# Softmax attention on one core: two heads' logits issued together on 64 array rows each, two masked blocks merged, one output bank

## The reference, cut to what matters

```python
for each head h, for q in blocks of 64 tokens:
    s_s = q[h] @ k_sel.T * scale + bias[h];   o_s = masked_softmax(s_s) @ v_sel
    s_w = q[h] @ k_win.T * scale + bias[h];   o_w = masked_softmax(s_w) @ v_win
    y[h] = gate0 * o_c + gate1 * o_s + gate2 * o_w
# second block, 8 heads
    y2[h] = masked_softmax(q2[h] @ k2[h].T * scale) @ v2[h]
```

## Time and profile before

| | |
|---|---|
| median of 3 runs | 2138.66 us (2137.55 to 2139.3) |
| time of the profiled execution | 2139.25 us |
| its span, first to last instruction | 2137.4 us |
| PE busy in the span | 1762.5 us (82%) |
| DVE, ACT, POOL busy | 757.8, 482.0, 224.2 us |
| mean granted TensorE clock | 0.909 of full speed |
| selected block, from POOL's first copy to DVE's last addition | 309.7 to 365.3 us |
| window block, likewise | 365.7 to 423.2 us |
| moba block | 1401.0 to 1455.0 us |

### The profile page before, as it was taken

One profiled execution on the slowest core, in us unless ns is written; L12 is line 12 of the kernel. 1 busy time (PEld: TensorE's weight loads), 2 busy tenths in 40 slices (PEclk: granted clock), 3 DMA queues, 4 the chain that ended last, 5 costly groups with the idle time before them and its releaser, 6 DMA issues. The chain is left out here.

```text
span 2137.4 us, 21540 instructions
## 1 busy us (share of the span) xinstructions
PE 1762.5 (82%) x8022; PEld 1175.6 (55%) x8023; DVE 757.8 (35%) x1353; ACT 482.0 (23%) x804; POOL 224.2 (10%) x280
## 2 busy tenths in 40 slices
PE   4979998897778799979978996577539999998873
PEld 2768876755333677868866885356433333333331
DVE  6335225522453677323342122753241111111113
ACT  3212334433000322222222223342101011100001
POOL 4010001000102122200030000010201111110011
PEclk9999999989989899989999995788859999999996
DMA  9312210001560577222221320001909998799994
GB/s 285 111 59 79 87 52 1 1 0 52 204 231 22 207 250 254 80 79 98 98 79 59 99 79 1 1 0 59 361 16 392 425 425 333 315 425 427 426 424 171
DMA packets 99669, 361.52 MB, mean 169 GB/s; under 512 B 21239, under 2 KB 23459, under 8 KB 87275
## 3 DMA queue, kind: packets, MB, share of 16 engines
q1 hardware_dynamic: 90791, 344.48, 42.5%
q0 software_dynamic: 5760, 9.02, 1.2%
q10 hardware_dynamic: 3012, 6.59, 0.8%
HBM read 357.28 MB, written 14.75 MB: 174 GB/s over the span
## 5 line engine op out<-in xcount | busy, mean ns | idle before, releaser
L2299 PE MATMUL x_gpa<-x_ring,x_Ta 128*64 128x512 f32 x608 | 145.9, 636 | 17.6 <-DMA x_ring<-in_w_expert_gate_dram 16.0
L2299 PE MATMUL x_upa<-x_ring,x_Ta 128*64 128x512 f32 x608 | 139.0, 611 | 15.7 <-DMA x_ring<-in_w_expert_up_dram 15.7
L2299 PEld LDWEIGHTS x_gpa<-x_ring,x_Ta 128*64 128x64 f32 x608 | 49.1, 146 | 111.9 <-issue 111.8
L2299 PEld LDWEIGHTS x_upa<-x_ring,x_Ta 128*64 128x64 f32 x608 | 47.5, 141 | 105.2 <-issue 105.2
L317 DVE TENSOR_TENSOR p_lo<-p_raw,p_hi 128x2048 fp32r<-128x2048 f32 x18 | 41.3, 2292 | 145.3 <-ACT p_hi L670 145.3
L324 PE MATMUL fr_p<-p_hi,u_high 128*128 128x512 f32 x224 | 89.1, 398 | 0.0
L325 PE MATMUL fr_p<-p_lo,u_high 128*128 128x512 f32 x224 | 88.0, 393 | 0.0
L326 PE MATMUL fr_p<-p_hi,u_low 128*128 128x512 f32 x224 | 88.0, 393 | 0.0
L2320 PE MATMUL x_y0a<-x_ring,x_aTa 128*64 128x512 f32 x304 | 69.4, 598 | 6.2 <-ACT x_aTa L2360 3.6
L2355 ACT ACTIVATE x_siga<-x_gpa 128x512 f32<-128x512 f32 x19 | 11.3, 597 | 265.5 <-PE x_gpa L2299 265.5
L2320 PE MATMUL x_y1a<-x_ring,x_aTa 128*64 128x512 f32 x304 | 68.6, 592 | 0.0
(11 more groups left out here) (1008 smaller groups left out, 3881.4 us busy)
## 6 DMA issues: line engine op xcount, KB each, us to landing
x_ring<-in_w_expert_gate_dram SPq DMA_DIRECT2D x32, 2048.0 KB, 24.6
x_ring<-in_w_expert_up_dram SPq DMA_DIRECT2D x32, 2048.0 KB, 31.4
x_ring<-in_w_expert_down_dram SPq DMA_DIRECT2D x32, 2048.0 KB, 29.9
p_raw<-in_w_in_dram SPq DMA_DIRECT2D x18, 1024.0 KB, 5.1
adaw0m<-in_w_ada_dram SPq DMA_DIRECT2D x6, 2048.0 KB, 10.4
adaw1m<-in_w_ada_dram SPq DMA_DIRECT2D x6, 2048.0 KB, 9.7
fr_ada<-in_ada_w_dram SPq DMA_DIRECT2D x4, 2048.0 KB, 16.8
w_raw0m<-in_mlp_w_dram SPq DMA_DIRECT2D x8, 1024.0 KB
```

Source lines behind the costliest of these rows:

```text
L2299: mm = nc.tensor.matmul(ps[CAP * f:CAP * f + CAP, :], self.xT[:, k, CAP * f:CAP * f + CAP], w[m + f][:, k, :], start=(k == 0), stop=(k == ...
```

## The change

A new class `HeadPairs` takes the place of `Heads` in `softmax_attention` (the mLSTM stage keeps `Heads`).

- **Logits by pairs.** The scores of both heads of a unit are issued in one go, in the order of `PAIR_ORDER`, each over its own 64 rows of queries and keys, so that one head's matmuls use array rows 0 to 63 and the other's 64 to 127. Five banks hold the eight results; two of them share bank 4, and `shared` keeps the second of these behind the first. One semaphore step at the end of the pair says that all logits are there. The scores of pair p+1 are issued behind the first head of pair p and wait until all logits of pair p are read.
- **One block for both masked kinds.** The selected and the window branch are two `Branch` entries of one call: four heads in a unit, with queries and bias staged once for both.
- **One bank for outputs.** The outputs of the two heads lie in halves of one bank `ops`; the first weigh of a head waits until DVE has read the outputs of the head before (`out_read`).
- **Finish.** Reciprocal and gate are issued ahead of the wait for the last weigh.
- PE's program is written out for all units instead of a hardware loop.

```diff
+PAIR_BANK = [lambda h: 2 + h, lambda h: 4, lambda h: 2 + h, lambda h: h]
+PAIR_COL = [lambda h: 384, lambda h: 256 * h, lambda h: 0, lambda h: 0]
+
+PAIR_ORDER = [(0, 1), (1, 3), (0, 3), (1, 2), (0, 2), (1, 0), (1, 1), (0, 0)]
...
+class HeadPairs:
...
+        self.sps = [s.bank(f"sps{j}{tag}") for j in range(5)]
+        self.tps = [s.bank(f"tps{j}{tag}") for j in range(2)]
+        self.ops = s.bank(f"ops{tag}")
...
+        def scores(pair, i, first=False):
+
+            if not first:
+                pe.wait_ge(self.scores_read, 8 * pair)
+            for h, j in PAIR_ORDER:
+                r = slice(64 * h, 64 * h + 64)
+                if (h, j) == (1, 1):
+                    pe.wait_ge(self.shared, pair + 1)
+                mm = nc.tensor.matmul(self.logits_of(h, j), self.qst[r, P * j:P * j + P], self.keys_now(i, h, P * (j + 1))[r, :],
+                                      start=True, stop=True)
+                if (h, j) == (0, 1):
+                    mm.then_inc(self.shared, 1)
+            mm.then_inc(self.scores_ready, 1)
...
+        def weigh(n, h, i, br, j):
+            if j == 0:
+                pe.wait_ge(self.out_read, n + 1)
...
+        def unit(i, last):
+            for k, br in enumerate(self.branches):
+                pair = nb * i + k
+                head(2 * pair, 0, i, br)
+                if k + 1 < nb:
+                    self.keys_now = self.branches[k + 1].keys
+                    scores(pair + 1, i)
+                elif not last:
+                    self.keys_now = self.branches[0].keys
+                    pe.wait_ge(self.q_staged, i + 2)
+                    scores(pair + 1, i + 1)
+                head(2 * pair + 1, 1, i, br)
...
-def softmax_attention(nc, C, tag, qT, keys, values, out, units=4, bias=None, gate=None, add=False):
+def softmax_attention(nc, C, tag, qT, branches, units=4, bias=None):
...
+                def coefs(n, h, i, br):
                     ch = Chain(dve, own, n * links)
+                    dve.wait_ge(H.probs_ready, 4 * n + 4)
+                    dve.wait_ge(H.turned, 4 * n + 12)
+                    ch.link(nc.vector.reciprocal(coef[h][:, :], sums[h][:, :]))
+                    if gate:
+                        ch.link(nc.vector.tensor_tensor(coef[h][:, :], coef[h][:, :], br.gate(h, i), ALU.mult))
+                    return ch
+
+                def finish(n, h, i, br, pair):
+                    ch = coefs(n, h, i, br)
                     dve.wait_ge(H.weighed, 4 * n + 6)
...
+                    o = H.ops[:, 256 * h:256 * h + NT * HD].rearrange("p (t d) -> p t d", d=HD)
+                    to = tmp[:, :, :] if add else br.out(h, i)
+                    nc.vector.tensor_tensor(to, o, bcast(coef[h][:, :], HD), ALU.mult).then_inc(H.out_read, 1)
                     if add:
...
+                        dve.wait_ge(H.out_read, n + 2)
+                        ch.link(nc.vector.tensor_tensor(br.out(h, i), br.out(h, i), tmp[:, :, :], ALU.add))
                     assert ch.n == links
 
                 def rounds(now, nxt):
                     for j in range(NT):
                         if nxt:
-                            logits(nxt[0], nxt[1], j)
+                            if j == 0 and nxt[1] == 0:
+                                dve.wait_ge(H.scores_ready, nxt[4] + 1)
+                            logits(nxt[0], nxt[1], nxt[2], j)
...
-                        for tag, kz, branch in (("sl", B.ksz, 1), ("wn", B.kwz, 2)):
...
+                        softmax_attention(nc, C, "sw", lambda i: B.qT[:, bass.ds(i, 1), :].rearrange("p a n -> p (a n)"),
+                                          [branch(B.ksz, 1), branch(B.kwz, 2)],
+                                          bias=lambda half, i: C.bias[:, bass.ds(i + 4 * half, 1), :].rearrange("p a n -> p (a n)"))
...
```

More of the change, by code:

```diff
@@ L1275, in softmax_attention @@
         own = s.sem(f"own{tag}")
-        links = 1 + bool(gate) + bool(add) + 1
+        gate, add = bool(branches[0].gate), branches[0].add
+        links = 1 + gate + add
         with nc.Block() as block:
@@ L1279, in _ @@
             def _(pe):
-                H.pe(pe, C, units, keys, values)
+                H.pe(pe, C, units)
             @block.gpsimd
@@ L1290, in stage @@
                             if not first:
-                                pool.wait_ge(H.scores_read, 8 * i + 4 * half)
+                                pool.wait_ge(H.scores_read, 8 * len(branches) * i - 4 + 4 * half)
                             pool.tensor_copy(bst[half][:, :], bias(half, i)).then_inc(bias_staged, 1)
@@ L1300, in _, with logits @@
             def _(dve):
-                def logits(n, half, j):
+                def logits(n, h, i, j):
                     w = P * (j + 1)
@@ L1305, in logits @@
                         if bias:
[L1306 to L1311, removed]
@@ L1313, in finish @@
-                def finish(n, half, i):
-                    ch = Chain(dve, own, n * links)
+                            dve.wait_ge(bias_staged, 2 * i + h + 1)
+                        dve.sem_inc(begun, 1)
+                    nc.vector.tensor_tensor_reduce(H.probs[h][:, OFF[j]:OFF[j + 1]], H.logits_of(h, j),
+                                                   bst[h][:, P * (NT - 1 - j):512], 1.0, 3e38, ALU.add, ALU.min,
+                                                   low[h][:, j:j + 1]).then_inc(H.scores_read, 1)
@@ L1335, in rounds @@
                         finish(*now)
-                dve.sem_inc(H.scores_read, 4)
                 dve.sem_inc(H.copied[0], 1)
-                dve.sem_inc(H.head_out, 2)
+                dve.sem_inc(H.out_read, 1)
                 H.run(dve, units, rounds)
@@ L1347, in rounds @@
                         if nxt:
[L1348 to L1354, removed]
+                            n, h = nxt[0:2]
+                            act.wait_ge(H.scores_read, 4 * n + j + 1)
+                            p = H.probs[h][:, OFF[j]:OFF[j + 1]]
+                            nc.scalar.activation(p, p, ACT.Exp, scale=-1.0, bias=low[h][:, j:j + 1],
+                                                 accum_out=sums[h][:, j:j + 1]).then_inc(H.probs_ready, 1)
                 act.sem_inc(H.copied[1], 1)
@@ L2954, in program, with branch @@
                                   s3.twin("u1_low", "uT", [P, KD, TOK]))
-                        for tag, kz, branch in (("sl", B.ksz, 1), ("wn", B.kwz, 2)):
[L2956 to L2963, removed]
+                        def branch(kz, b):
+                            return Branch(lambda i, half, w: kz[:, half, 0:w],
+                                          lambda t, half, i: B.kv[:, t, 256 * b - 128 + 64 * half:256 * b - 64 + 64 * half],
+                                          lambda half, i: B.oa[:, :, bass.ds(i * 64 + 256 * half, 64)],
+                                          lambda half, i: B.ga[:, :, bass.ds(i * 3 + 12 * half + b, 1)].rearrange("p t a -> p (t a)"), add=True)
+                        softmax_attention(nc, C, "sw", lambda i: B.qT[:, bass.ds(i, 1), :].rearrange("p a n -> p (a n)"),
+                                          [branch(B.ksz, 1), branch(B.kwz, 2)],
+                                          bias=lambda half, i: C.bias[:, bass.ds(i + 4 * half, 1), :].rearrange("p a n -> p (a n)"))
                     stick_breaking(nc, C, B)
```

92 lines of the change are left out of this document (80 added, 12 removed).

## The result

The changed kernel takes 2155.99 us (median of 9 runs, 2148.09 to 2163.22) against 2138.66 (9 runs beside it, 2137.10 to 2141.68). The ratio is 1.0084, with a 95% interval of 1.0064 to 1.0103: slower by 17.3 us. The forecast was slower by 40.4, and 2162 as the lower end of its own case. The profiled execution took 2161.49, 5.5 above the median, so its trace shows more than the median loses: 22.3 us of span.

What follows compares the result with a forecast made beforehand. PE seemed the bound, with DVE's path nearly as long, so halved logits become a wait for DVE. Full-clock terms -2.0 - 6.7 + 3.0 - 1.2 = -7 us, clock falls +47.4: +40.4, 2179 us; range 2130 to 2206.

Steps and rivals of the forecast that it cites:

- its own case: Main forecast: the clock falls at each odd-to-even step; 2179 us, range of its own 2162 to 2202, chance 0.51.
- merge: Selected and window branches in one block: -6.7 us, of which 1.4 are half clock in the selected block's last head.
- the forecast's upper bound: 2202 us, if the pair needs 3 slots more or drains cost 0.3 at a switch between 64 and 128 rows.
- I take it that the clock falls at each: At odd-to-even steps, 7 merged and 3 moba, PE idles 1.85 to 2.15 us and the clock falls; 4.4 a pair.
- may give 0.3 more: Moba, without gate and addition, might gain 0.3 us more than the general step estimate.
- clock: Half-clock cost: +33.1 us in the merged block plus +0.9 for its last head, +13.4 in moba; together +47.4.
- start: First logits on DVE wait for the whole pair: +2.0 us in the merged block, +1.0 in moba.
- steps: Two steps between heads take 7.75 against 7.96 us: -0.2 for each of 10 pairs, -2 in all.
- end: Block ends: hoist, -0.6 us, and -0.6 in the last steps.
- The clock holds: Rival: the clock falls in at most one of ten odd-to-even steps; 2131.7 us, chance 0.17.
- Falls in some steps only: Rival: the clock falls in two to six of ten steps; 2138 to 2160 us, chance 0.15.
- The third rival: Halves do not run side by side, or the clock does not return in the scores; 2215, serial 2260; chance 0.17.

Runs made afterwards that it cites:

- e1: Changed kernel plus 12 identity transposes on PE before each even head's first weigh (but the first) in the masked block; 2136.99 us.
- e3: Changed kernel with each masked head's addition moved on DVE behind the next head's first copy, and DVE's program written out; 2122.58 us.
- e11: The deferred-addition kernel (2122.58) with scores over all 128 rows, so the two halves run one after the other; 2144.28 us.
- e5: The deferred-addition kernel (2122.58) with two more additions into a scratch tile on DVE behind each moba head's scaling; 2144.82 us.
- e10: The kernel with both first copies moved ahead (2124.10), plus 9 and 2 identity transposes on PE in each block's first head; 2120.24 us.
- e9: The kernel with DVE's first copy moved ahead (2147.21), with ACT's first copy also ahead of the next head's first exponential; 2124.10 us.
- e2: Kernel before the change with only the selected and window branches merged into one block, scores head by head; 2131.52 us.
- e12: The merge-only kernel (2131.52, no pairs) with the addition deferred and DVE's program written out; 2136.91 us.
- e6: Changed kernel with only DVE's program written out for all units instead of a hardware loop; 2149.89 us.
- e7: Changed kernel with the selected and window branches as two calls again, keeping pairs and one output bank in each; 2166.16 us.
- e8: The deferred-addition kernel (2122.58) with DVE's first copy of a head ahead of the next head's first logits tile; 2147.21 us.
- e4: Changed kernel with scores over all 128 rows of the zero-padded keys, in the same order; 2170.27 us.

## Why the prediction was right in direction and more than twice too large

**Right.** The bound moved as said: the scores had hidden `finish`, and without them PE waits for DVE. The pair of scores took 2.42 (2.5 forecast). In the masked block the idle was 1.53 to 2.18 (1.85 to 2.15 forecast; five of the seven were 1.75 or less), released by DVE's copy each time, the clock fell at all seven steps, and three pairs (350.57 to 401.57, last weigh to last weigh) lasted 16.87, 17.25 and 16.88 (16.5 to 17). With the clock held, e1's pairs lasted 12.42 and 12.79, so a fall costs 4.45 (4.4). The merge gave 8.2 alone (6.7). The switch from 128 to 64 rows, 0.3 in the forecast's upper bound, costs some 0.1: the pair of scores starts 1.03 behind the start of the last weigh in e3 (334.52 to 335.55), the scores over 128 rows 0.94 in e11 (336.03 to 336.97).

**The step that failed: "I take it that the clock falls at each".** The forecast priced ten falls with one idle. For moba I wrote that missing gate and addition "may give 0.3 more", and left its idle at 1.85 or more. Its step takes 2.65 against 3.19 in a masked unit and 3.6 between units; its idle is 1.21, 1.18 and 0.81, and the clock held at all three steps. e5 shows that it would have fallen at 1.98. By my terms, with half of the ends in either block, moba was to lose 13.2 us (13.4 of clock, 1.0 at the start, less 0.6 in steps and 0.6 at the end); it lost 0.6. The half clock in its first head cost 4.1 (e10 against e9), a fall that the forecast had not priced: it was luck that this made the miss smaller by a quarter. Without it moba gained 3.5: its full-clock pair is 11.69 instead of 12.63. The nearest row was there: moba's own idle of 1.00 where the masked ones had 1.66 and 1.67. A chain that is 0.66 shorter at the block's end is shorter inside it, too. The half clock at moba's start was outside the window of the earlier trace rows, which opens at 1407.50; from its first scores on the block's clock before was 0.97 and not 1.00.

**The masked block was 7.2 too large as well:** +27.3 by my terms (34.0 of clock, -6.7 merge, -1.4 steps, +2.0 start, -0.6 end), +20.15 measured. *Start:* the 2.0 did not come. The first weigh stands 5.64 behind POOL's first copy, against 5.83 before (315.55): before, PE issued the second head's scores ahead of the first turning, and the pair takes that time away as it adds its own. Moba's start (6.58 after the first scores against 6.75) likewise. *Clock:* one of the seven falls was short. The head that began at 332.66 had its last eight passes in 1.06 again, and the pair from there (336.31 to 350.57) lasted 14.26 instead of 17.25: 3 less. *Merge:* e2 has 1.5 more than its term. Together 6.7 of the 7.2. Taking moba's 12.6 and the 7.2 here off the forecast's 40.4, and adding the 1.5 of the other stages, leaves the 22.3 of the trace but for rounding.

**The rivals.** "The clock holds" was wrong in the masked block and right in moba's three steps, and its price of 4.4 a fall was right (4.45). Its time, 2131.7, was not reached by e1, where the clock held at all ten steps: 2136.99, with both blocks' first heads and the masked block's last one still at half clock. e3_defer is below it, but with a shorter chain on DVE. The Trainium skill (TensorE: Matmul & The Clock Gate, Why this matters for your kernels) warns of longer gaps; the traces here disagree, with falls behind 1.52 to 2.18. "Falls in some steps only" gave 2138 to 2160 for two to six of ten. 2156 lies there, but the trace has seven of ten: the number fits better than the count. The third rival was wrong in both halves: the scores run side by side, 2.42 against 4.53 for the same work in turn (e11), and the clock came back with each pair of scores: they ran at half clock (403.41 to 408.05), and the odd head behind them at full (409.14, two passes in 0.41). That matmuls on different row groups run concurrently, as the Trainium skill says (same page, Part 3: Packing small matmuls), the traces now show for rows.

**The median** is 5.5 below the profiled execution, and the nine runs spread over 15 us against 4.6 for the kernel before (9.4 in its 22 runs beside e9 to e12). The traces of e6, e7 and e8, in which five steps fell and one or two with the same idle did not, make it likely that the number of falls differs from run to run. The mean granted clocks of the nine fit that: 0.901 in the fastest run, 0.891 and 0.893 in the two slowest, though the order between is not strict. Which steps fell in them is not shown, since there is one trace.

## What to carry to other kernels

When an edit takes work off the bounding engine, work out the idle that it leaves for each stage by that stage's own chain, not by the worst one: here moba's 1.2 us cost nothing and the masked block's 1.5 to 2.2 cost up to 4.45 each. Shorten the other engine's chain first: here one addition behind a copy instead of ahead of it, and DVE's loop written out, turned a loss of 0.8% into a gain of 0.8% (2122.58). And look at what stands behind a moved instruction on every engine: e8 let one copy of each head start 0.2 us sooner and lost 25.

## What the runs showed of the hardware

**The clock has no sharp edge in the idle.** Odd-to-even steps, by their idle: 1.98, 3 of 3 fell (e5, moba); 1.53 to 2.18, 7 of 7 (changed); 1.73 to 2.09, 5 of 6 (e7); 1.52, 5 of 7 (e6); 0.54 and 0.81 together, 5 of 7 (e8); 0.81 to 1.24 in moba, none of 12 (changed, e1, e4, e7); 0.75 in the masked block, 3 of 21 (one each in e3, e5 and e11), and in moba none of 9 (e3, e6, e11). A step at the same idle fell or held in the same block. The step to a block's last head, which has no scores in it either, says the same: in the masked block the clock fell behind 1.12 and 1.13 (e1, e4, e6) and held behind 1.20 (e12). So the length of one idle does not decide alone, and what else does stays open.

**A longer stretch of scores ahead of the idle often holds it, but not always.** The first head fell behind scores of 2.42 and an idle of 1.12. Behind scores one after the other and idles of 1.10 to 1.11 it held in three of four cases: in both blocks of e4 and in the masked one of e11 (4.6 us of scores). In e11's moba it fell (eight passes in 1.91 at 1416.78), behind 6.4 us of scores, 3.6 of them at half clock.

**The clock also moves stages that are the same.** Behind a wait of 12 us, the first eight matmuls of `mx` took, before and changed (PE's timeline):

```profile
541.58 5.15 PE L1579 MATMUL mx<-wu,oT 128*128 128x512 f32 x8 [11.99 <-PEq L1515]
546.57 3.60 PE L1579 MATMUL mx<-wu,mT 128*128 128x512 f32 x8
```

```profile
562.45 6.63 PE L1720 MATMUL mx<-wu,oT 128*128 128x512 f32 x8 [12.45 <-PEq L1656]
```

At full clock eight take 3.60. The granted clock came back some 3 us behind the first matmul before (in the microsecond from 544) and some 6 behind it in the changed kernel (from 568), which cost 1.5 us. From the first matmul of `stick_breaking` to moba's first scores one execution each took 977.99 (before), 981.20 (changed), 982.37 (e1) and 976.08 (e3): 6 us between programs with the same instructions there, more than the 4.3 that I had called indistinguishable for the whole kernel. Whether the program ahead or the single execution makes the difference is not shown.
